# Four experts' down weights loaded during the output projection, and two late modulation products re-placed on TensorE

## The reference

```
mod = silu(c) @ w_ada + b_ada                  # 6 x 1024 values, for c and for c_ctx
xn  = rmsnorm(x) * (1 + sc1) + sh1             # adaLN
x   = x + g1 * (concat(conv(xn), retention(xn)) @ w_out)       # "output projection"
t   = rmsnorm(x) * (1 + sc2) + sh2
gates = top-1 of 4 groups, then top-2 of 8 experts             # "router"
x   = x + g2 * sum_e gates[:, e] * ((silu(t @ w1_e) * (t @ w3_e)) @ w2_e)   # 32 experts
y   = rmsnorm(x)
```

## Time and profile before

| | |
|---|---|
| median of 3 runs | 697.33 us (695.92 to 697.91) |
| profiled execution, its own time | 695.76 us |
| its span in the trace | 693.9 us |
| PE busy | 586.9 us, 85% of the span |
| DVE / ACT / POOL busy | 45% / 20% / 21% |
| DMA, mean | 257 GB/s; 419 to 422 GB/s in every slice (17.35 us) from 451 to 642 us, 30 or 31 GB/s in the three from 312 to 364 us |
| mean granted TensorE clock | 0.94 of full speed |

### The profile page before, as it was taken

One profiled execution on the slowest core, in us unless ns is written; L12 is line 12 of the kernel. 1 busy time (PEld: TensorE's weight loads), 2 busy tenths in 40 slices (PEclk: granted clock), 3 DMA queues, 4 the chain that ended last, 5 costly groups with the idle time before them and its releaser, 6 DMA issues.

```text
span 693.9 us, 8564 instructions
## 1 busy us (share of the span) xinstructions
PE 586.9 (85%) x3496; PEld 394.9 (57%) x3496; DVE 311.8 (45%) x619; ACT 140.3 (20%) x269; POOL 145.3 (21%) x113
## 2 busy tenths in 40 slices
PE   3799999999999989899999758999888877788800
PEld 3579999888888856544554425555444433443300
DVE  1432228623602357524677636665433333334347
ACT  5334531121322333301111120111000100000012
POOL 0043642424242100020000021232222222121200
PEclk9999999999999999999999669999988999999955
DMA  7985231130330399770006899999999999999484
GB/s 276 387 296 200 71 122 53 69 122 0 122 116 6 124 369 328 256 289 30 31 31 231 361 347 400 363 422 419 419 419 420 420 419 420 420 420 420 177 317 186
DMA packets 47482, 178.67 MB, mean 257 GB/s; under 512 B 5624, under 2 KB 5800, under 8 KB 34768
## 3 DMA queue, kind: packets, MB, share of 16 engines
q1 hardware_dynamic: 39116, 155.83, 57.0%
q0 software_dynamic: 7360, 19.63, 7.8%
q10 hardware_dynamic: 964, 2.63, 1.1%
HBM read 170.17 MB, written 14.19 MB: 266 GB/s over the span
## 4 chain that ended last, share of the span: by engine, by line
PE 66%; DMA 21%; DVE 6%; ACT 3%; SPq 2%; issue 2%; DVEq 0%; POOLq 0%; ACTq 0%
DMA ring<-in_w_up_e 17%; PE bank L963 9%; PE bank L964 9%; PE bank L1137 9%; PE bank L965 9%; PE bank L1252 9%; PE bank L1272 4%; PE bank L922 3%; PE bank L939 2%; PE bank L1244 2%; PE bank L1154 2%; DMA ring<-expert_out_rows 1%; PE bank L1017 1%; SPq L461 1%; SPq L465 1%
## 5 line engine op out<-in xcount | busy, mean ns | idle before, releaser
L1252 PE MATMUL bank<-ring,arena_ab 128*64 128x256 f32 x416 | 104.5, 409 | 27.5 <-DMA ring<-in_w_up_e 23.7
L1256 PE MATMUL bank<-ring,arena_ab 128*64 128x256 f32 x416 | 104.6, 409 | 0.0
L1252 PEld LDWEIGHTS bank<-ring,arena_ab 128*64 128x64 f32 x416 | 59.7, 148 | 76.4 <-DMA ring<-in_w_up_e 36.8
L572 POOL TENSOR_TENSOR w_lo<-ring,w_hi 128x1024 fp32r<-128x1024 f32 x25 | 61.3, 2452 | 112.6 <-ACT w_hi L723 112.6
L643 POOL DMA_INDIRECT expert_out_rows<-arena_ab,row_out x32 | 40.1, 1254 | 130.4 <-DVE arena_ab L1356 130.4
L1356 DVE TENSOR_TENSOR arena_ab<-arena_ab,bank 64x256 f32<-64x256 f32 x32 | 19.6, 613 | 106.3 <-ACT arena_ab L879 106.2
L963 PE MATMUL bank<-xn_hi,w_hi 128*128 128x320 f32 x192 | 61.6, 321 | 3.7 <-DVE xn_lo L1356 3.6
L963 PE MATMUL bank<-w_hi,xn_hi 128*128 128x512 f32 x160 | 63.3, 396 | 0.0
L964 PE MATMUL bank<-w_lo,xn_hi 128*128 128x512 f32 x160 | 62.9, 393 | 0.0
L965 PE MATMUL bank<-w_hi,xn_lo 128*128 128x512 f32 x160 | 62.8, 392 | 0.0
L1256 PEld LDWEIGHTS bank<-ring,arena_ab 128*64 128x64 f32 x416 | 59.7, 148 | 0.0
(11 more groups left out here) (235 smaller groups left out, 903.3 us busy)
## 6 DMA issues: line engine op xcount, KB each, us to landing
ring<-in_w_gate_e SPq DMA_DIRECT2D x26, 1024.0 KB, 26.3
ring<-in_w_up_e SPq DMA_DIRECT2D x26, 1024.0 KB, 28.0
ring<-in_w_down_e SPq DMA_DIRECT2D x26, 1024.0 KB, 26.7
ring<-in_w_ada SPq DMA_DIRECT2D x11, 2048.0 KB, 12.8
ring<-in_w_in SPq DMA_DIRECT2D x6, 2048.0 KB, 8.2
arena_ab<-in_w_gate_e SPq DMA_DIRECT2D x6, 1024.0 KB, 25.8
arena_ab<-in_w_up_e SPq DMA_DIRECT2D x6, 1024.0 KB, 27.5
arena_ab<-in_w_down_e SPq DMA_DIRECT2D x6, 1024.0 KB, 26.2
```

Of the source, the lines that this page charges most:

```text
L572: pool.tensor_tensor(as_piece(w_lo[p_ % 2], p_), piece_of(w, p_), as_piece(w_hi[p_ % 2], p_), ALU.subtract).then_inc(w_lo_ready, 1)
L1252: pe.matmul(bank[2 + p_][0:BLK, 0:DE], lhs, w_gate(s)[:, kt, :], start=(kt == 0), stop=(kt == KT - 1))
L1256: last = pe.matmul(bank[2 + p_][BLK:2 * BLK, 0:DE], lhs, w_up(s)[:, kt, :], start=(kt == 0), stop=(kt == KT - 1))
```

## The change

Three things are changed.

1. SP loads the down weights of experts 0, 1, 2 and 4 (4 MiB, into the last thirds of slots 1, 2, 0 and 3) as soon as the retention is through and the rows are back, ahead of all gate and up weights. The waits for modulation rows 10 and 11 are dropped from its queue. So that the last thirds are free, `late_sum` moves to `arena_b`.
2. In the output projection's loop, tile 1 does `project(1, 1)` before `router_T(0)`, where all other tiles do it behind `router_T`.
3. `late_mod(1)` writes `bank[0]`, not `bank[2]`, and is cut in two halves of four matmuls: one behind `late_mod(0)`, one behind `slots(3)` and ahead of `late_mod_row(0)`.

```diff
-        late_sum = [tail[0][:, 0:512], tail[3][:, 0:512]]
+        late_sum = [arena_b[:, 7168 + SL * n:7168 + SL * n + SL] for n in range(len(LATE_MODS))]
...
-            for n in range(2):
+            sp.wait_ge(o_mm, NT)
+            sp.wait_ge(yT_mm, NT)
+            sp.wait_ge(modrow_ev, len(ROW_MODS))
+            for n in (0, 1, 2, 4):
+                down_of(n)
+            for n in range(3):
                 released(sp, e_slot[n], FIRST_EXPERT_ITEM)
                 gate_up_of(n)
-                down_of(n)
-
-            released(sp, e_slot[2], FIRST_EXPERT_ITEM)
-            gate_up_of(2)
...
-            sp.wait_ge(modrow_mm, 7)
-            down_of(2)
-
             released(sp, e_slot[4], FIRST_EXPERT_ITEM)
-            sp.wait_ge(modrow_mm, 8)
             sp.wait_ge(xe_in[0], 16)
             sp.wait_ge(xe_in[1], 16)
             gate_up_of(4)
-            down_of(4)
...
                 project(t, 0)
+                if t == 1:
+                    project(t, 1)
                 if t >= 1:
                     router_T(t - 1)
...
-                project(t, 1)
+                if t != 1:
+                    project(t, 1)
...
-                if n == 0:
-                    pe.wait_ge(x1_ready, 2 * (NT - 1))
-                pe.wait_ge(mod_ev, s)
-                landed(pe, N_IN + s)
+                if steps[0] == 0:
+                    pe.wait_ge(x1_ready, 2 * NT - 2 + n)
+                    pe.wait_ge(mod_ev, LATE_MODS[0])
+                    landed(pe, N_IN + s)
...
-                    last = pe.matmul(bank[2][32 * j:32 * j + 32, :], cs[:, kt, :], w[:, kt, :],
+                    last = pe.matmul(bank[2 - 2 * n][32 * j:32 * j + 32, :], cs[:, kt, :], w[:, kt, :],
...
-            late_mod(0)
+            late_mod(0, range(KT))
+            late_mod(1, range(HALF_K))
             router_T(NT - 1)
             slots(NT - 3)
             ranks(NT - 2)
             router(NT - 1)
             slots(NT - 2)
+            late_mod(1, range(HALF_K, KT))
             late_mod_row(0)
-            late_mod(1)
             ranks(NT - 1)
```

More of the change, by code:

```diff
@@ L822, in late_mod_sum @@
                 act.wait_ge(mod_mm, LATE_MODS[n] + 1)
-                act.activation(late_sum[n][0:SUM_ROWS, :], bank[2][0:SUM_ROWS, :], ACT.Copy).then_inc(mod_ev, 1)
+                act.activation(late_sum[n][0:SUM_ROWS, :], bank[2 - 2 * n][0:SUM_ROWS, :], ACT.Copy).then_inc(mod_ev, 1)
             def late_mod_row(n):
@@ L1192, in _, with late_mod @@
                     ranks(t - 2)
-            def late_mod(n):
+            def late_mod(n, steps):
                 s = LATE_MODS[n]
-                if n == 0:
-                    pe.wait_ge(x1_ready, 2 * (NT - 1))
-                pe.wait_ge(mod_ev, s)
-                landed(pe, N_IN + s)
+                if steps[0] == 0:
+                    pe.wait_ge(x1_ready, 2 * NT - 2 + n)
+                    pe.wait_ge(mod_ev, LATE_MODS[0])
+                    landed(pe, N_IN + s)
                 w = wide(N_IN + s)
-                for kt in range(KT):
+                for kt in steps:
                     j = kt % 4
-                    last = pe.matmul(bank[2][32 * j:32 * j + 32, :], cs[:, kt, :], w[:, kt, :],
+                    last = pe.matmul(bank[2 - 2 * n][32 * j:32 * j + 32, :], cs[:, kt, :], w[:, kt, :],
                                      start=(kt < 4), stop=(kt >= 4))
-                last.then_inc(mod_mm, 1)
+                if steps[-1] == KT - 1:
+                    last.then_inc(mod_mm, 1)
             def late_mod_row(n):
```

## The result

The changed kernel takes 694.06 us (median of 20 runs, 690.37 to 696.32), the kernel before on the same chip 697.72 us (20 runs, 694.75 to 699.27). The ratio is 0.9946 (95% interval 0.9932 to 0.9961), or 3.7 us less; 693.7 us were predicted. The profiled execution of the changed kernel has a span of 692.9 us, only 1.0 us less than that of before. Why one profile shows less than the medians is part of what follows.

A forecast was written before the change was run, and what follows sets the result against it. The bound was taken as PE's way to expert 1's down products (436.58 us), then 213.2 us of weight stream. Terms 0.83 + 1.2 + 1.6 = 3.6 us took 697.33 to 693.7 us; range 690.0 to 696.8 us.

The forecast's parts named there:

- The two-part bound: Up to 436.58 us PE's way to expert 1's down products binds; after it the bytes issued from there, 213.2 us.
- Rival A: Weight stream: it never ran dry, so the 4 MiB count in full, 10.0 us less, 687.3 us; chance 4%.
- Expert 6's load as the end of the first part: Expert 6's down load moves from 436.58 to 432.9 us, with the DMA idle ahead of it for longer than before.
- the prediction's own signs of being wrong: DMA not idle ahead of expert 6's load, clock differing from 385 to 433 us, or new waits after ranks(4).
- Tile 1's order: Output projection: PE's 1.66 us wait ahead of router_T(0) goes, a 0.83 us wait behind it comes; gain 0.83 us.
- late_mod(1) in the wait: Its first half hides in PE's 4.58 us wait for tile 4's norm, taking 0.96 us and leaving 3.6.
- ranks(4): PE starts it earlier, with only half of late_mod(1) ahead (2.63 us), until DVE's choose(4) limits; gain 1.2 us.
- The first gather: Issued at 402.0 us on a free DMA, it takes 3.7 us instead of 5.37; gain 1.6 us, at most 1.8.
- From the first transpose on, PE, DVE and the clock repeat what they did: From the experts' first transpose on nothing changes, so expert 6's down load comes at 432.9 us and 213.2 us follow.
- rival D: Experts' start: PE stays at 1.2 GHz into expert 0, 8.1 us more, so slower at 701.8 us; chance 8%.
- Rival B: Tile 4: the clock stays at 2.4 GHz through router_T(4) and router(4), 2.0 us more gain, 691.7 us; chance 10%.
- Rival C: Hardly anything arrives: slow row writes, gather meets weights, ranks(4) gains nothing; 0.83 to 1.8 us, 696 us; chance 20%.

The follow-up runs named there:

- PE's order alone: The kernel before with only tile 1's new order and late_mod(1) in two halves, down loads where they were: 696.24 us, ratio 0.9979.
- the repeat: The changed kernel run once more, nothing altered, for a second profile: 692.63 us, ratio 0.9935 to the kernel before.
- the early loads alone: The kernel before with only the early down loads and late_sum moved, PE's order as before: 694.61 us, ratio 0.9973.
- the late bytes: The changed kernel with the down weights of experts 20 to 23 (4 MiB) not loaded: 683.94 us, ratio 0.9807 to the kernel before.
- the release order on before: The kernel before, from expert 5 on loading gate and up of n + 1 ahead of down of n: 690.16 us, ratio 0.9901.
- the last experiment: The changed kernel with ten unread PE products and loads in the order slots come free: 686.49 us, ratio 0.9842 to the kernel before.
- the release order on the changed kernel: The changed kernel, from expert 5 on loading gate and up of n + 1 ahead of down of n: 687.91 us, ratio 0.9869.
- the extra products alone: The changed kernel with ten unread products of 512 columns put into PE's waits: 690.06 us, ratio 0.9891 to the kernel before.

## Why the prediction was right, and where it was not

**The two-part bound: right.** Four early MiB gave 1.9 us, four late ones 10. From expert 6's down load to the last weights it was 213.22, 212.92 and 213.3 us, and 202.95 us with 4 MiB less behind it. Rival A is out.

**Expert 6's load as the end of the first part: wrong for the changed kernel.** "With the DMA idle ahead of it, for longer than before" did not come: the share there is 1.03, and the last pause lies one load group earlier, where the missing bytes opened it (246 GB/s from 426.0 us before, none now). So two of the prediction's own signs of being wrong came, this one and a clock that differs between 385 and 433 us, without the rivals that they were to announce. The first part now ends with expert 5's down load; from there to the last weights it is 221.92 us (223.90 before). The stretch from there to expert 6's down load was shorter (9.00 instead of 10.68 us), so the next loads arrived before the stream had emptied. In the trace of before the clock was at 0.50 from 429.5 to 433.5 us, in expert 2's products, and in the changed kernel it was not. The same window of the kernel before:

```profile
431.00:431.50 0.50, 0.50 (x4) 0.30 (x2) 0.00 (x0) 0.00 (x0) 0.17 (x1) 0.50 1.17 492
```

and of the changed one:

```profile
431.00:431.50 0.50, 0.50 (x8) 0.41 (x6) 0.18 (x1) 0.00 (x0) 0.50 (x1) 1.00 1.13 475
```

**Tile 1's order: right.** 0.88 us for 0.83; the wait behind the first `router_T` is 0.74 us.

**late_mod(1) in the wait: right.** The wait is 3.72 us for 3.6.

**ranks(4): right, then lost by half.** To `ranks(4)` the gain is 12.53 - 11.24 = 1.29 us for 1.2, bound by `choose(4)`. Two sizes behind it were off by nearly 1 us each and cancel: the half product took 1.73 us, not 2.63, the row products 1.91, not 0.95. But before, the long run of `late_mod(1)` had brought the clock up at 399 us, and `ranks(4)` and `slots(4)` ran at 2.4 GHz (0.41 us); cut in half, they run at 1.2 (0.64 us). From `ranks(4)` to the gather it is 0.65 us more. The term comes to 0.64.

**The first gather: right.** 5.37 - 3.79 = 1.58 us for 1.6. The fifth row write landed within 6.7 us at the most (6.0 were argued, 8.5 before), and the DMA was idle at 405.5 us. The cap was real as well: DVE's wait has shrunk to 0.18 us. On an idle DMA the way from issue to PE was 3.62 to 3.83 us in six profiles. By the Trainium skill's page "DMA: Bandwidth & Descriptors" (section "Anatomy of one DMA — SWDGE (gpsimd) path") I had an estimate of 3.2 us, less than any of these. One reading beside the term was wrong: "a gather never waits for the whole of the weights ahead". When the gather was issued, 8.6 us after the first of these weights, only some 3 us of them were left, so its 5.37 us could not bear that out; and the queues of the kernel before and of PE's order alone show it standing until the weights were nearly through. Whatever turns the queues take by the rule cited there, here the measurement decides.

**"From the first transpose on, PE, DVE and the clock repeat what they did": the step that failed.** It failed twice, in opposite directions. The clock came up at 417.9 us instead of 416.0, and expert 0's stretch took 0.92 us more: rival D, in small. And the 1.7 us in expert 2 went. Without these the terms come to 0.88 + 0.64 + 1.58 = 3.1 us; with them 3.1 - 0.9 + 1.7 = 3.9, and 3.7 were measured between medians. Less the 3.1 us of slow clock ahead of it in this profile, the gather went out at 402.5 us (402.0 forecast) and expert 6's down load at 432.7 (432.9). The forecast of 3.6 is right in its terms to some tenths, except for `ranks(4)`, which lost half; it owes part of its nearness to luck, because what it missed nearly cancels.

**Rival B** did not come by itself: in the repeat, with the early loads alone and with the late bytes PE came back before the clock had fallen, but then it waited 0.75 to 0.87 us for DVE's `place`, the clock fell, and `router` ran at half speed. Kept busy by force, it gave the 2 us it was priced at. **Rival C** is out by the time. **Rival D** was of the right kind: a cold start of the experts is a real price, 3.4 us in the changed kernel by the run that removes it, of which before already paid 2.5. The rule behind it, by the Trainium skill's page "TensorE: Matmul & The Clock Gate" (section "Part 1: The HAM clock gate"), that sustained activity lifts the clock, agrees with that run: with products ahead of the transposes the clock was 1.00 from 402 us on.

**Open:** why the stretch at 1.2 GHz in expert 2 comes and goes. The kernel before, PE's order alone, the release order on before and the last experiment have it, and there it is 10.7 us from expert 5's to expert 6's down load; the changed kernel twice, the early loads alone, the late bytes, the release order on the changed kernel and the extra products alone do not, and there it is 9.0. So all three profiles without the early loads have it, and of the seven with them only the last. A link with the early loads is therefore possible, but not shown. If there is one, these 1.7 us are a gain of the change that the prediction did not have; if not, they are chance of single executions, and the 3.9 us above are no account of the 3.7 between medians.

## What to carry to other kernels

Before bytes are moved out of a full stream, find the last window in which it was empty: bytes ahead of it are worth only what else they hold up (here a gather), bytes behind it count in full. An in-order issuing queue should take its waits in the order in which they end: that edit alone gave 7 us, twice what the careful placing of loads and products gave. And a product moved out of a dense run can take the clock from the short ones behind it, so price what follows it at both clocks.

## What the runs showed of the hardware

- The granted clock fell to 0.50 for 3 to 4 us in the middle of dense products of 512 columns (373.5 to 377 us in the changed kernel, 372 to 376 with the early loads alone), at different places in different executions, and cost PE 1.6 to 1.7 us each of these times: the first half of `project(4, 1)` took 5.38 and 5.29 instead of 3.68 us.
- A gather of 512 KB needs 3.62 to 3.83 us from issue to its reader when the DMA is idle, and 4.46 to 5.91 us beside weights in flight. There its queue moved no packet until the weights were nearly through (1.05 MB of weights and none of the gather from 404.0 to 406.5 us in the kernel before), and PE had the rows a good 2 us after that. In PE's order alone it came earlier and took longer.
- Extra products of the same kind helped or hurt by the clock at which they ran. Four from 383 us on, at 2.4 GHz, preceded a `router_T` and a `router` at full speed. Two from 397 us on, at 1.2 GHz, took 3.76 us and delayed `slots(4)`, and the clock came up only behind them, at 402 us; the same two from 398.6 us on, at 2.4 GHz in the last experiment, took 1.96 us and delayed nothing.
